# A two-layer streaming encoder step on one core: both key-value heads of the windowed attention in one step, laps of six units, and other banks, slots and orders around them

## What is computed

```python
h = _rmsnorm(x, p['g_pre_mix'])
(qn, qr, ckv, kr, qb, kb, vb, qc, kc, vc, alr, gc, gate) = _split_cols(h @ p['w_in'])
oa = ...   # A: latent attention, 8 heads, all earlier chunks visible
ob = ...   # B: 8 query heads over 2 key-value heads, window of 128, ALiBi, sinks
oc, s = _gla_branch(qc, kc, vc, alr, gc, s0, p)   # C: gated linear attention, 4 heads
y = (g[..., 0, :] * (oa @ p['w_up_a']) + g[..., 1, :] * (ob @ p['w_up_b'])
     + g[..., 2, :] * (oc @ p['w_up_c']))
x = x + _rmsnorm(y @ p['w_out'], p['g_post_mix'])
f = jnp.square(jax.nn.relu(_rmsnorm(x, p['g_pre_mlp']) @ p['w_ff1'])) @ p['w_ff2']
x = x + _rmsnorm(f, p['g_post_mlp'])
```

## Time and profile before

| | |
|---|---|
| median of 3 runs | 2501.56 us (2493.05 to 2506.61) |
| the profiled execution | 2499.4 us, of which the span from the first to the last instruction is 2497.3 us |
| PE, share of the span busy | 96% |
| DVE, ACT, POOL | 38%, 40%, 43% |
| HBM traffic | 73 GB/s over the span |

### The profile page before, as it was taken

One profiled execution on the slowest core, in us unless ns is written; L12 is line 12 of the kernel. 1 busy time (PEld: TensorE's weight loads), 2 busy tenths in 40 slices (PEclk: granted clock), 3 DMA queues, 4 the chain that ended last, 5 costly groups with the idle time before them and its releaser, 6 DMA issues.

```text
span 2497.3 us, 41989 instructions
## 1 busy us (share of the span) xinstructions
PE 2397.2 (96%) x17852; PEld 2229.9 (89%) x17852; DVE 955.4 (38%) x1810; ACT 990.5 (40%) x1879; POOL 1064.1 (43%) x653
## 2 busy tenths in 40 slices
PE   6999999999999899999979999999999998999997
PEld 6899977888789899999979999788887998999997
DVE  3455554543632601000464555445356225010014
ACT  4344333333345552423344443344334555424322
POOL 3444313443456364544333342144434563545442
PEclk9999999999999999999999999999999999999999
DMA  4111231112124032222321113211211241222222
GB/s 165 43 60 58 79 92 51 52 52 72 46 60 166 33 93 85 85 85 77 102 73 56 60 58 91 68 52 52 68 59 43 68 147 60 85 85 85 85 77 80
DMA packets 58937, 187.74 MB, mean 75 GB/s; under 512 B 7872, under 2 KB 16800, under 8 KB 58112
## 3 DMA queue, kind: packets, MB, share of 16 engines
q1 hardware_dynamic: 48608, 164.33, 21.0%
q10 hardware_dynamic: 10144, 20.73, 2.6%
HBM read 170.87 MB, written 10.89 MB: 73 GB/s over the span
## 4 chain that ended last, share of the span: by engine, by line
PE 88%; DVE 6%; ACT 3%; POOL 1%; issue 1%; DMA 0%; ACTq 0%; SPq 0%; DVEq 0%; POOLq 0%
PE dense L787 47%; PE att L787 22%; PE att L833 2%; PE att L1023 2%; PE att L1085 2%; PE att L972 1%; PE att L909 1%; PE att L895 1%; PE att L988 1%; PE att L1057 1%; PE att L913 1%; DVE h_raw L1679 1%; PE att L1039 1%; DVE h_lo L1668 1%; DVE x L1652 1%
## 5 line engine op out<-in xcount | busy, mean ns | idle before, releaser
L2025 POOL TENSOR_TENSOR wlo<-wraw,whi 128x1024 fp32r<-128x1024 f32 x302 | 729.7, 2422 | 938.5 <-ACT whi L1154 938.3
L787 PE MATMUL dense<-h_hi,whi 128*128 128x280 f32 (+1 forms) x2256 | 677.3, 300 | 34.1 <-DVE q_cat L1578 7.8
L787 PE MATMUL dense<-h_lo,whi 128*128 128x280 f32 (+1 forms) x2256 | 666.2, 295 | 0.0
L787 PE MATMUL dense<-h_hi,wlo 128*128 128x280 f32 (+1 forms) x2256 | 665.0, 295 | 0.0
L787 PEld LDWEIGHTS dense<-h_hi,whi 128*128 128x128 f32 (+1 forms) x2256 | 432.6, 192 | 60.6 <-issue 31.0
L787 PEld LDWEIGHTS dense<-h_hi,wlo 128*128 128x128 f32 (+1 forms) x2256 | 431.8, 191 | 1.3 <-issue 0.5
L787 PEld LDWEIGHTS dense<-h_lo,whi 128*128 128x128 f32 (+1 forms) x2256 | 431.8, 191 | 0.0
L1154 ACT ACTIVATE whi<-wraw 128x1024 fp32r<-128x1024 f32 x302 | 315.4, 1050 | 289.3 <-DMA wraw<-in_w 272.1
L787 PE MATMUL att<-h_hi,whi 128*128 128x280 f32 (+1 forms) x784 | 231.7, 295 | 9.0 <-DVE h_lo L1668 5.0
L787 PE MATMUL att<-h_lo,whi 128*128 128x280 f32 (+1 forms) x784 | 230.4, 294 | 0.0
L787 PE MATMUL att<-h_hi,wlo 128*128 128x280 f32 (+1 forms) x784 | 230.3, 294 | 0.0
(11 more groups left out here) (306 smaller groups left out, 4635.2 us busy)
## 6 DMA issues: line engine op xcount, KB each, us to landing
wraw<-in_w SPq DMA_DIRECT2D x302, 512.0 KB, 3.6
x_spill<-x ACTq DMA_DIRECT2D x2, 2240.0 KB, 7.5
x<-x_spill ACTq DMA_DIRECT2D x2, 2240.0 KB, 12.1
k_cat<-k_rope ACTq DMA_DIRECT2D x16, 212.0 KB, 3.5
x<-in_x SPq DMA_DIRECT2D x4, 560.0 KB, 6.2
out_y_out<-x SPq DMA_DIRECT2D x4, 560.0 KB, 3.1
out_c_out<-ckv ACTq DMA_DIRECT2D x2, 560.0 KB, 7.0
const<-in_const SPq DMA_DIRECT2D x1, 1112.0 KB, 12.1
```

Of the source, the lines that this page charges most:

```text
L787: mm = pe.matmul(bank(u, o, hf)[0:m, :], a[:, k, o * 128:o * 128 + m], b[:, k, H[hf]], start=(k == 0 and i == 0), stop=(k == kt - 1 and i ...
L2025: pool.tensor_tensor(wlo[slot][:, :], wraw[slot][:, :], whi[slot][:, :].bitcast(F32), ALU.subtract).then_inc(pool_done, st.done("pool", f" ...
```

## The change

1. `LAP` is 6 instead of 5; the plan's places for sums and mean squares follow (`LAP - 2`). A layer's first eight units take their slots from `EDGE` first, then `BASE`; the last six of `ff2` from `MLP`, `BASE` and one of `EDGE`. With one more unit done by halves, all of C runs one unit later in the list.
2. The first head of C has a dense unit on each side of the step that squares `ckv`. `p lev 0` no longer waits for the previous head's `rstd`: `p ms` writes M_ and O_, and `p lev 1` waits instead. In `p lev 0` the smaller level of a pair goes first.
3. In the last head, `silu` comes one unit earlier, before the unit `qr` 0 instead of after `kv`. The two state DMAs are issued at the start of `v o`, for every head. DVE's wait for them moves from `qn` 0 to `qn` 1. The 13 `prep_a` steps stand after four units instead of six, and one unit (`up_c` 0) lies between them and the first scores.
4. Dense banks: four (two more: M_ and O_) from `qn` 1 to `up_c` 0; three (M_) from `qb` 1 up to `out`. PE waits at `qn` 1 for the last head's `rstd`, and at the first scores of A for the copies of the lent banks.
5. B has five steps of four parts. Scores of both heads go to four banks, products of the two heads alternating. DVE computes for each head bias, sink, largest and its negative multiple; the subtraction is now the bias operand of ACT's exponential. Meta and previous-chunk keys lie side by side, so that one transpose of up to 80 columns takes both. Values alternate between the heads. The list is: scores, dense, sums and values of i-1, turn of head 0, half unit, turn of head 1, half unit.
6. `prep_b` gathers meta and previous values by two ACT copies and turns them by three transposes. The distance table is loaded in a permuted order.

```diff
-LAP = 5
+LAP = 6
-                        for j in (next(norms) for _ in range((2, 1, 1, 0, 0)[i])):
+                        for j in (next(norms) for _ in range((2, 1, 1, 0, 0, 0)[i])):
...
-                for steps in ((1, 2), (3, 4), (5, 10, 11), (6, 7, 8), (9, 12), (13,)):
+                for steps in ((1, 2), (3, 4, 5), (10, 11, 6), (7, 8, 9, 12, 13), ()):
                     dense()
                     order.extend([("prep_a", s) for s in steps])
...
-                for j in range(len(JOBS["b"]) + 2):
-                    order.append(("att", "b", j))
+                for i in range(5):
+                    order.append(("b", i, "scores"))
                     dense()
+                    order.append(("b", i, "sums"))
+                    if i > 0:
+                        order.append(("b", i - 1, "values"))
+                    order.append(("b", i, "turn 0"))
+                    u = next(dn)
+                    order.extend([("half", u, 0), ("b", i, "turn 1"), ("half", u, 1)])
+                order.append(("b", 4, "values"))
...
-                return [*BASE, *EDGE] if u in V_NEXT else [*BASE]
+                return [*EDGE, *BASE] if u < LAP + 2 else [*BASE]
...
-                b = min(SIX if wide else TWO, key=lambda c: bank_free[c])
+                b = min(SIX if wide else FOUR if UIDX["qn", 1] <= u <= UIDX["up_c", 0] else THREE if UIDX["qb", 1] <= u < UIDX["out", 0] else TWO, key=lambda c: bank_free[c])
...
+                    if kind == "qn" and n == 1:
+                        pe.wait_ge(act_done, A("act", f"gla rstd {C_HEADS - 1}"))
...
-                        if h > 0:
-                            pe.wait_ge(act_done, A("act", f"gla rstd {h - 1}"))
                         pe.wait_ge(act_done, A("act", f"gla z {h}"))
...
-                        pe.wait_ge(act_done, A("act", f"gla oevac {h - 1}" if h > 0 else "prep a 0"))
+                        pe.wait_ge(act_done, A("act", f"gla rstd {h - 1}" if h > 0 else "prep a 0"))
...
-                            mm = pe.matmul(ps[:, S0 + hf, 0:HALF], c_("ones_v"), gsq[:, 0, H[hf]], start=True, stop=True)
+                            mm = pe.matmul(ps[:, (M_, O_)[hf], 0:HALF], c_("ones_v"), gsq[:, 0, H[hf]], start=True, stop=True)
...
+                    for g in range(B_G):
+                        qc = slice(128 * i, 128 * i + 128) if i < 4 else slice(META0, T)
+                        rows = P if i < 4 else MIXED
+                        for n_ in range(2):
+                            for t in range(2):
+                                r64 = slice(64 * t, 64 * t + 64)
...
+                                mm = pe.matmul(ps[0:rows, OWN[t] + g // 2, c0:c0 + key.shape[1]], qb[r64, g, qc], key,
+                                               start=(g % 2 == 0 and n_ == 0), stop=True, skip_group_check=True)
...
+                def b_turn(i, t):
+                    pe.wait_ge(pool_done, A("pool", f"b prob {i} {t}"))
...
+                            pe.transpose(ps[0:n, PREV[t], c], pb[:, g, 0:n], c_("ident"))
+                            mm = pe.transpose(ps[:, OWN[t], c], pb[:, g, n:n + 128], c_("ident"))
...
-                                if kind == "qn" and n == 0 and hf == 0:
+                                if kind == "qn" and n == 1 and hf == 0:
                                     dve.wait_ge(stored, STORES * l + 32 * C_HEADS)
...
+                def b(i, what, up):
+                    rows = P if i < 4 else MIXED
+                    if what == "scores":
...
+                        for t in range(2):
...
+                            link(dve.tensor_reduce(sm[:, 4:8], pb[:, :, :], AX.X, ALU.max))
+                            dve.tensor_scalar(sm[:, 0:4], sm[:, 4:8], -B_SCALE, None, ALU.mult).then_inc(dve_done, st.done("dve", f"b max {i} {t}"))
+                            if t == 0 and up is not None:
+                                evac(up, [0], (0, 1))
+                    if what in ("scores", "sums"):
+                        t = 0 if what == "scores" else 1
+                        sm = stat[0:rows, t, :]
+                        dve.wait_ge(act_done, A("act", f"b exp {i} {t}"))
+                        dve.reciprocal(sm[:, 12:16], sm[:, 8:12]).then_inc(dve_done, st.done("dve", f"b rsum {i} {t}"))
...
+                def b(i, what):
+                    if what in ("scores", "sums"):
+                        t = 0 if what == "scores" else 1
+                        pool.wait_ge(dve_done, A("dve", f"b rsum {i} {t}"))
...
+                        pool.tensor_tensor(pb, pb, rs, ALU.mult).then_inc(pool_done, st.done("pool", f"b prob {i} {t}"))
```

More of the change, by code:

```diff
@@ L552, in program @@
                 if step[0] == "half":
-                    halves.append((l_, step[1], 0, step[2]))
+                    halves.extend([(l_, step[1], o, step[2]) for o in range(outs_of(UNITS[step[1]][0])[0])])
                 elif step[0] == "dense":
@@ L826, in gla @@
                             pe.wait_ge(dve_done, A("dve", f"gla lev {h} {i}"))
-                            for n_, m in enumerate(pair):
+                            for n_, m in ((1, pair[1]), (0, pair[0])):
                                 e = level_of(m)
@@ L833, in gla @@
                                     mm = pe.matmul(ps[0:rows, PAIR_BANK[i], c0:c0 + 64].rearrange("p (g t) -> p g t", t=m),
-                                                   e[:, 128 * sb:128 * sb + rows], late, start=(n_ == 0 and sb == 0), stop=True,
+                                                   e[:, 128 * sb:128 * sb + rows], late, start=(n_ == 1 and sb == 0), stop=True,
                                                    skip_group_check=True)
@@ L1106, in prep_b @@
                             pe.transpose(ps[:, T0, 128 * i:128 * i + 128], vb[:, 128 * i:128 * i + 128], c_("ident"))
[L1107 to L1108 removed]
+                        pe.wait_ge(act_done, A("act", "b keys"))
                         for i in range(3):
[L1110 to L1111 removed]
@@ L1128, in _ @@
                         prep_b(step[1])
+                    elif step[0] == "b":
+                        if step[2] == "scores":
+                            b_scores(step[1])
+                        elif step[2] == "values":
+                            b_values(step[1])
+                        elif step[2].startswith("turn"):
+                            b_turn(step[1], int(step[2][-1]))
                     elif step[0] == "att":
@@ L1166, in evac @@
                     if kind.startswith("gate"):
-                        act.wait_ge(*sig_free(kind[-1], n))
-                        for hf in range(2):
+                        if hfs[0] == 0:
+                            act.wait_ge(*sig_free(kind[-1], n))
+                        for hf in hfs:
                             s = sig[:, n % 2, H[hf]]
@@ L1340, in gla @@
                     if s == "v o":
+                        for which, slot in (("p_state", 5), ("s_state", 7)):
+                            act.wait_ge(dve_done, A("dve", f"gla state {h}"))
+                            act.dma_start(io[which][bass.ds(l * C_HEADS + h, 1), :, :].rearrange("a p n -> (a p) n"), state[:, slot, :]).then_inc(stored, 16)
+                            count["stored"] += 16
                         act.wait_ge(pe_done, A("pe", f"gla o {h}"))
@@ L1612, in evac @@
                     for o in range(outs_of(kind)[0] if outs != [0] else 0):
-                        if kind in ("up_a", "up_b") and y_engine(kind[-1], n + o) == "dve":
+                        if kind in ("up_a", "up_b") and hfs[-1] == 1 and y_engine(kind[-1], n + o) == "dve":
                             dve.wait_ge(dve_done, A("dve", f"evac {u} {o} 1"))
@@ L1979, in _, with leads @@
+                def leads(step):
+                    return step[0] == "att" or (step[0] == "b" and step[2] == "scores")
                 for at_step, (l, step) in enumerate(order):
@@ L1981, in _ @@
                     if step[0] == "dense":
-                        early = order[at_step - 1][1][0] == "att" and UNITS[step[1]][0] in ("up_a", "up_b")
+                        early = leads(order[at_step - 1][1]) and UNITS[step[1]][0] in ("up_a", "up_b")
                         evac(step[1], [1] if early else None, (0, 1))
@@ L2038, in evac @@
                         lo_tile(s[1][:, n % 8, c], s[0][:, n % 8, c], s[2][:, n % 8, c], f"hid lo {n}" + end, f"hid hi {n}" + end)
-                    if kind in ("up_a", "up_b"):
+                    if kind in ("up_a", "up_b") and hfs[-1] == 1:
                         for o in range(2):
```

293 lines of the change are left out of this document (163 added, 130 removed).

## The result

The changed kernel takes **2482.6 us** (median of 4 runs, 2477.5 to 2484.2) where the kernel before took 2500.3 beside it: ratio 0.993, 95% interval 0.991 to 0.995, 17 to 18 us less. The forecast was 2463. The direction and the range held; the gain was less than half of the 39 us forecast.

The account below looks back on a forecast made before the run. The prediction took PE, busy 96% of the span, as the bound. Its terms summed to -38.8 us, taking the profiled 2499.4 to 2460.6 and the median to 2463 us, with a range of 2425 to 2492.

Parts of the forecast that it names:

- B: Stage B: 32.5 us less PE work a layer, mostly eaten by new waits for POOL's product; -4 us in all.
- laps with their clock: Laps: mean-square waits vanish after `out`, 0.3 to 0.5 stays after `ff2`; -12 us, and -3 for the lower clock.
- start of C: Start of C: two `w lo` waits go, unit 7 waits for unit 6's bank instead; -13 us.
- `rstd` at head 1: Wait before `p lev 0` of head 1 goes, 1.5 us and a restart each; -3.7 us.
- `oc_hi`: Four waits for a bank behind DVE's output go, since ACT copies that bank's new content; -5 us with one clock drop.
- `q_cat`: Last head: the waits for the `q_cat` copies go with four banks; -12 us with the clock.
- step 5 of the preparation: Last head: prep 5 waits 3.5 to 5.6 us for prep 3's copy on DVE; +13 us, bounds 0 and +17.
- `rstd` at `qn` 1: Last head: PE waits at `qn` 1 for `rstd`, with one more ACT instruction than the removed wait; +4.2 us.
- Rival 2: B: POOL's product of head 1 is not behind `w lo`, so waits and clock loss go; 2401 us, chance 0.13.
- Rival 1: B: score pairs of the two heads do not overlap; +10.8 us, less shorter waits, 2472 us; chance 0.18.
- Rival 4: B: five waits a layer leave PE at 1.2 GHz for most of it; +60 us a layer, 2580; chance 0.10.
- rival 3: Laps: DVE's full list and a `w lo` holding it keep all six waits; 2478 us, chance 0.11.

Follow-up runs that it names:

- e4: Changed kernel with, in B, the weight-tile split moved from behind the dense unit to behind POOL's product for the second head: 2436.6 us, ratio 0.975.
- e4b: Changed kernel with, in B, the second head's reciprocal on DVE and product on POOL ahead of the dense unit in all lists: 2420.6 us, ratio 0.969.
- e5b: Changed kernel with B's score products in the order of before, all 16 of head 0 and then all 16 of head 1: 2491.8 us, ratio 0.996.
- e7: Changed kernel with the nine `w lo` subtractions of POOL planned into the laps replaced by fills with zeros: 2472.8 us, ratio 0.990.
- e1: Changed kernel with the six units of the next layer's first stage fixed to PSUM banks 0 to 5 in both layers: 2473.4 us, ratio 0.990.
- e2: Changed kernel with each lap's three weight-tile splits moved, one ahead of the next norm's sums and two after its tokens: 2476.0 us, ratio 0.991.
- e5: Changed kernel with two inner loops of B's scores exchanged, so the heads take turns two products at a time: 2483.6 us.
- e6: Changed kernel with the last five groups of A's preparation divided as before the change, a unit again between steps 4 and 5: 2473.4 us, ratio 0.990.

## Why the prediction was too good

The terms of the sum beside what they measured, both layers (B and `prep_b` from the windows, the rest as losses of before and after):

| term | forecast | measured |
|---|---|---|
| B | -4 | -4.2 |
| `prep_b` | -2.4 | -1.7 |
| laps with their clock | -15 | -4.9 |
| start of C | -13 | -4.5 |
| `rstd` at head 1 | -3.7 | -3.7 |
| `oc_hi` | -5 | -5.2 |
| `silu` | +1.4 | +0.5 |
| `q_cat` | -12 | -12.1 |
| step 5 of the preparation | +13 | +17.7 |
| `rstd` at `qn` 1 | +4.2 | +6.0 |
| `va` | -2.3 | -2.0 |
| the kernel's start (not in the sum) | 0 | -2.6 |
| sum | -38.8 | -16.7 (spans: -16.2) |

**B was right in mechanism and size.** Scores of both heads 2.46 (forecast 2.3), eight transposes of a head 0.9, values of both 2.0, a new stretch of 199.3 and 200.7 (forecast 200.5). PE's waits for `prob` in layer 0 are 2.0, 5.45, 4.77, 2.44 and 5.50 us for i = 0 to 4 (forecast 2.9, 6.4, 4.9, 4.5 and 5.1), and 22.4 a layer in all (forecast 24). Two small errors cancel in that: i = 3 came out at half its size, and the turns of head 0 at i = 0, 1 and 3, called covered, waited 0.73, 0.58 and 0.88. The chain was read from the order of the lists alone, and e4 and e4b took it apart. One link was not named: the prediction put POOL's product behind `w lo`, `w hi` and the gate on ACT, but DVE's reciprocal stands behind the gate too, and e4b against e4 shows 16 us for it. A wait of 5.45 us lost 7.6 with the clock behind it, 2.2 beyond itself, as priced. Rival 2, POOL's product free of `w lo`, was priced at 62 us. The edit that does just this is e4, and it gained 46; the 62 of e4b need the reciprocal moved as well, so what the price fits is the whole wait with its clock, and not the `w lo`. Rival 1 is dead in this order of products; its price of 10.8 was near e5b's 9 only by luck, as 1.7 us a step would be 15 of work. Rival 4, the clock staying low, did not come: 0.94 and 0.93 in B.

**Laps: the term was mis-sized by 10 us.** The failed step is "after `out` they vanish; after `ff2` ... 0.3 to 0.5 stays". Of six waits, three fell to 0.2 or nothing and three stayed at 1.70, 1.40 and 1.67, and the first `h_lo` behind `out` in layer 0 waits 2.34 where it had waited 0.87. A lap of six has room for one more half unit and also for more weight tiles to split (nine `w lo` in the three laps instead of five), and I had counted the half unit and not the splits. It stood among the rivals: rival 3 names the `w lo` that holds DVE. The forecast took all of it or none, and half of it happened. e7 gives the size: 13.5 us by losses, 9.8 in the time.

**Start of C: the step "unit 7 waits for the bank of unit 6" holds for one layer only.** In layer 0 it came out to the hundredth (2.2 forecast, 2.20 measured, 3.95 lost with the clock). I worked out the banks for layer 0 and took them for both. In layer 1 unit 6 waits for `cv` 1, the very wait that I wrote of as gone: 10.35 lost instead of 3.95, and e1 gives back 6 there.

**Step 5: the mechanism was right, its size short.** DVE's work was read rightly: from the copies of `kra` to the end of the head's output 12.8 us, a `w lo` in it:

```profile
316.79 0.73 DVE L1865 TENSOR_TENSOR kra<-kra,const 32x560 f32<-32x560 f32 x1
...
325.91 2.90 DVE L1852 SCALAR_TENSOR_TENSOR oh<-oh,par,rstd 128x560 f32<-128x560 f32 x1
...
332.05 0.74 DVE L1867 TENSOR_TENSOR rtmp<-att,const 128x560 f32<-128x560 f32 x1
```

From the start of prep 1 (315.64) PE needs 11.1 us, until 326.70, where I had 11.5; DVE has the copy that prep 5 waits for after 17.2 us, at 332.80, where I had 17.1. So it waits 6.15 and not 5.6 at most. A stretch of 6.8 us at 0.50 begins in the wait and runs on behind it, and 8.3 and 9.4 are lost. The `w lo` did fall into the output (2.90 us instead of 0.80), so the low end of the wait, 3.5, was out, and the upper bound of the term (+17) was the right value; the +13 lay between the two.

**`rstd` at `qn` 1** waits 2.0 us as thought, but a stretch at the lower clock (3.4 us at 0.50) follows in layer 0, 1.5 more.

Errors of 10.1, 8.5, 4.7, 1.8 and twice under 1 us on one side, and of 4 on the other (2.6 of it the kernel's start), make the 22. The terms that were copied from a wait in the trace (`q_cat`, `oc_hi`, `rstd` at head 1) and B held within 0.3 us each; those that said what comes instead were short. The shorter start of the kernel (2.6) is no more than the same code scatters by: eight experiments (e1, e2, e4, e4b, e5, e5b, e6, e7) leave the start as it is in the changed kernel, and the products of `z` in layer 0 begin between 50.6 and 53.5 us in them, 50.61 in the changed kernel itself. So it can't be put down to the change. What isn't settled: what laps of six are worth by themselves, and why the low stretches of B fall as they do from run to run.

## What to carry over

When an edit gives a lap or a stage one more unit, list what comes along with the unit on every engine (its split, its copy, its bank) before counting the wait as gone; a planner that takes the least recently used bank or slot can give layer 1 another answer than layer 0, so read the assignment of each layer. When work on the bound engine is cut, the gain is what the other engines' lists let through: here 33 us of PE's work a layer were free, but one step in the wrong place in three lists (`sums` behind the unit) kept some 30 of them. Put the short step that the bound engine waits for ahead of the long one that nobody waits for.

## What the runs showed of the hardware

- Score products of two heads, in different 64 partitions, ran together in neighbouring order (32 in 2.46 us, starts of a pair 7 ns apart), and as well in twos (2.57); with all 16 of one head first, 4.21 (4.14 from start to start, where one head alone took 2.29), so only the products around the place where the heads meet overlapped, 0.4 us in all.
- A fill by POOL of 128x1024 took 0.95 us and did not hold up the DVE instruction beside it (`mix` 0.50, its usual time), the subtraction of the same shape took 2.4 us and held DVE for its length (the same `mix` 2.65, an `h_lo` 2.38 instead of 0.43).
- The clock came back after each long wait of B: in layer 0 a stretch of 6.8 us at 0.50 began within or at the end of the waits of 5.45, 4.77 and 5.50 us, one of 3.4 us behind that of 2.44, none at that of 2.00, and full speed followed each. The same waits gave 27.3 us at 0.50 in layer 1 of the changed kernel and 17.1 in e1 and e6.
